# The head's row scaling shared between VectorE and GpSimd

## The reference

```
h = rmsnorm(x, g_mix);  z = h @ w_in                 # w_in: 2048 x 5632
rmsnorm(x, g) = x * rsqrt(mean(x*x) + 1e-6) * g
mixer A: 16 heads x 64, three dilated windows, mixed by their softmax denominators
mixer B: 16 query heads / 4 kv heads x 64, window 128, with a sink logit per head
x1 = x + concat(A * silu(gate_a), B * silu(gate_b)) @ w_out
x2 = x1 + (p @ w_ple) * sigmoid(rmsnorm(x1, g_ple) @ w_pg)
y  = rmsnorm(x2, g_final)                            # and the keys and values of both mixers
```

## Time and profile before

| what | value |
|---|---|
| median of 3 runs | 2525.15 us (2521.14 to 2525.96) |
| the profiled execution's own time | 2522.66 us |
| its span in the trace | 2520.9 us |
| mean granted clock of PE | 0.989 of full speed |
| PE busy | 2427.4 us (96%) |
| DVE busy | 861.3 us (34%) |
| ACT busy | 634.7 us (25%) |
| POOL busy | 812.4 us (32%) |

### The profile page before, as it was taken

How to read it: one execution, slowest core, us unless ns; L and a number is a source line. 1 busy time by engine, 2 the same in 40 slices (tenths; PEclk the granted TensorE clock), 3 DMA queues, 4 the chain that set the end, 5 groups by cost and what they waited for, 6 DMA issues and landing times.

```text
span 2520.9 us, 41153 instructions
## 1 busy us (share of the span) xinstructions
PE 2427.4 (96%) x16473; PEld 2260.6 (90%) x16473; DVE 861.3 (34%) x2199; ACT 634.7 (25%) x1748; POOL 812.4 (32%) x858
## 2 busy tenths in 40 slices
PE   5999999999999999999999999999999999999986
PEld 4998888888888999888888899999999998999986
DVE  7022333333333322445545535251221253222242
ACT  6022222222222222333555510130000032112211
POOL 1322222222222222222212223333333233454896
PEclk9999999999999999999999999999999999999998
DMA  5232222223222214444434445352332343333675
GB/s 182 72 115 94 88 90 96 82 84 109 86 89 91 89 58 126 124 128 138 146 114 142 124 148 161 112 179 86 99 97 79 117 157 106 111 105 109 181 227 175
DMA packets 349110, 297.26 MB, mean 118 GB/s; under 512 B 22191, under 2 KB 314263, under 8 KB 347631
## 3 DMA queue, kind: packets, MB, share of 16 engines
q1 hardware_dynamic: 312197, 253.37, 33.1%
q10 hardware_dynamic: 36723, 41.26, 4.8%
HBM read 228.43 MB, written 66.12 MB: 117 GB/s over the span
## 4 chain that ended last, share of the span: by engine, by line
PE 82%; DVE 5%; POOL 5%; DMA 4%; ACT 1%; issue 1%; SPq 1%; DVEq 0%; POOLq 0%; ACTq 0%
PE psum L935 22%; PE psum L937 22%; PE psum L936 22%; PE psum L739 3%; PE psum L755 3%; PE psum L767 3%; POOL w_lo L708 3%; POOL w_hi L706 2%; DMA s_ring<-in_cache_a_k 2%; PE psum L795 1%; PE psum L823 1%; PE psum L810 1%; DVE x_n L1381 1%; DMA w_raw<-in_w_ple 1%; DVE s_prod L1474 1%
## 5 line engine op out<-in xcount | busy, mean ns | idle before, releaser
L935 PE MATMUL psum<-act_hi,w_hi 128*128 128x344 f32 x4032 | 1323.5, 328 | 21.0 <-POOL w_lo L708 11.3
L937 PE MATMUL psum<-act_hi,w_lo 128*128 128x344 f32 x4032 | 1290.7, 320 | 0.0
L936 PE MATMUL psum<-act_lo,w_hi 128*128 128x344 f32 x4032 | 1290.0, 320 | 0.0
L935 PEld LDWEIGHTS psum<-act_hi,w_hi 128*128 128x128 f32 x4032 | 762.0, 189 | 35.6 <-POOL w_lo L708 14.6
L706 POOL CAST w_hi<-w_raw 128x512 fp32r<-128x512 f32 (+1 forms) x390 | 246.9, 633 | 1652.7 <-PE psum L937 1505.1
L936 PEld LDWEIGHTS psum<-act_lo,w_hi 128*128 128x128 f32 x4032 | 761.6, 189 | 0.2
L937 PEld LDWEIGHTS psum<-act_hi,w_lo 128*128 128x128 f32 x4032 | 760.8, 189 | 0.0
L708 POOL TENSOR_TENSOR w_lo<-w_raw,w_hi 128x512 fp32r<-128x512 f32 (+1 forms) x390 | 503.8, 1292 | 31.2
L1404 DVE COPY prob_t<-psum 128x512 f32<-128x512 f32 (+2 forms) x96 | 53.5, 558 | 468.9 <-PE psum L767 468.9
L1155 ACT ACTIVATE prob_t<-psum 128x512 f32<-128x512 f32 (+2 forms) x96 | 47.1, 491 | 352.5 <-PE psum L767 352.5
L1161 ACT ACTIVATE prob<-prob,mx 128x256 f32<-128x256 f32 (+7 forms) x128 | 98.4, 770 | 147.0 <-DVE mx L1432 147.0
(11 more groups left out here) (192 smaller groups left out, 1900.0 us busy)
## 6 DMA issues: line engine op xcount, KB each, us to landing
w_raw<-in_w_in SPq DMA_DIRECT2D x208, 256.0 KB, 3.1
w_raw<-in_w_pg SPq DMA_DIRECT2D x94, 256.0 KB, 2.9
w_raw<-in_w_out SPq DMA_DIRECT2D x64, 256.0 KB, 2.7
z_scratch<-stage ACTq DMA_DIRECT2D x72, 172.0 KB, 1.8
h_scratch<-h_row ACTq DMA_DIRECT2D x16, 516.0 KB, 2.7
x_in<-in_x_prompt SPq DMA_DIRECT2D x8, 1024.0 KB, 4.9
zq<-z_scratch SPq DMA_DIRECT2D x32, 256.0 KB, 4.0
bias<-in_c_biasa SPq DMA_DIRECT2D x16, 512.0 KB, 4.2
```

Source lines behind the costliest of these rows:

```text
L935: pe.matmul(psum[:, bank, 0:T3], hi_w, hi_a[:, k, rows], start=(k == 0), stop=False, skip_group_check=True)
L936: pe.matmul(psum[:, bank, 0:T3], hi_w, lo_a[:, k, rows], start=False, stop=False, skip_group_check=True)
L937: return pe.matmul(psum[:, bank, 0:T3], lo_w, hi_a[:, k, rows], start=False, stop=stop, skip_group_check=True)
```

## The change

POOL takes columns 1408 to 2047 of each row tile's scaling and does it in two instructions. The first multiplies `x_in` by `g_row` into `x_n`; it waits for `x_squared`, since ACT writes its junk there. The second multiplies that by the inverse root, and waits for the DVE's `dve_chain` count of that tile's fourth small step. Both count `x_shared`. DVE's scaling keeps columns 0 to 1407. SP's load of tile i and PE's turning of a tile now wait for both counts. In POOL's program tiles 0, 1 and 2 stand ahead of weight group 0; tile 3 stands ahead of group 2, tile 4 ahead of group 3, and tiles 5 to 8 ahead of group 4.

```diff
+X_SHARE = 11 * P
@@ SP: loads of the row tiles
                 if i >= 2:
                     sp.wait_ge(sem("x_normed"), i - 1)
+                    sp.wait_ge(sem("x_shared"), 2 * (i - 1))
                 sp.dma_start(x_in[0:n, i % 2, :], x_p[r0:r0 + n, :] if i < 8 else x_s).then_inc(sem(f"x_loaded{i % 2}"), 16)
@@ POOL
+            def x_share(i):
+
+                r0, n = ROW_TILES[i]
+                pool.wait_ge(sem("x_squared"), i + 1)
+                pool.tensor_tensor(x_n[0:n, i % 2, X_SHARE:D], x_in[0:n, i % 2, X_SHARE:D], g_row[0:n, X_SHARE:D], ALU.mult).then_inc(sem("x_shared"), 1)
+                pool.wait_ge(sem("x_shared"), 2 * i + 1)
+                pool.wait_ge(sem("dve_chain"), 4 * i + 4)
+                pool.tensor_scalar(x_n[0:n, i % 2, X_SHARE:D], x_n[0:n, i % 2, X_SHARE:D], small[0:n, 18 + i:19 + i], None, ALU.mult).then_inc(sem("x_shared"), 1)
+
+            pool.wait_ge(sem("consts"), 64)
+            for i in range(3):
+                x_share(i)
             for g, (what, i, k, n) in enumerate(GROUPS):
+                for x in {2: (3,), 3: (4,), 4: (5, 6, 7, 8)}.get(g, ()):
+                    x_share(x)
@@ PE, x_turn
                 pe.wait_ge(sem("x_normed"), i + 1)
+                pe.wait_ge(sem("x_shared"), 2 * i + 2)
@@ DVE
-                dve.scalar_tensor_tensor(x_n[0:n, i % 2, :], x_in[0:n, i % 2, :], small[0:n, 18 + i:19 + i], g_row[0:n, :],
+                dve.scalar_tensor_tensor(x_n[0:n, i % 2, 0:X_SHARE], x_in[0:n, i % 2, 0:X_SHARE], small[0:n, 18 + i:19 + i], g_row[0:n, 0:X_SHARE],
                                          ALU.mult, ALU.mult).then_inc(sem("x_normed"), 1)
```

## The result

Over 11 runs of each kernel the median went from 2523.43 to 2535.11 us, 11.7 us more; the ratio of the times is 1.0048 with a 95% interval of 1.0038 to 1.0059. The forecast was 2534.2 us, slower, which is 9 us above the median of the three runs of before (2525.15 us). The profiled execution of the changed kernel took 2536.74 us, with a span of 2534.9 us, a granted clock of 0.986, PE busy 2427.6 us and POOL 854.5 us (42 more than before).

What follows compares the result with a forecast made beforehand. DVE bounds the head and PE the rest; the late x 3 costs tile 3 8.5 us, later tiles win nothing back, and PE passes tile 8 +9.4 late, taken as +9: 2525.15 + 9 = 2534.2 us, range 2526 to 2539.

Steps and rivals of the forecast that it cites:

- the held load: SP's queue: x 3 stands behind g 2, which waits for group 0's split behind tile 2; issued 8.9 us later.
- The main case: Head ends later through the late x 3 and mutual waits: +9 us, own range +6 to +11, chance 0.62.
- POOL is dearer: Rival: POOL's one-input product costs 1.54 us, or POOL gets ahead of DVE's scaling; +13 or about +12 us, chance 0.18.
- signs of being wrong: x 3 before 28 us, tiles at 5.2 us, POOL's scaling above 1 us, PE's clock lower behind the longer pause.
- The queue step: SP's order x 2, g 2, x 3: x 3 issued at 31.85 instead of 22.96 us, tile 3 scaled 8.5 late.
- The mutual wait: DVE instructions with two SBUF operands and POOL instructions exclude each other to the end; five tiles take 30.0 us against 29.5.
- the guess who goes first: Both scalings are released by the same count; DVE taken to go first, POOL following 1.65 us later.
- The mis-sized term: POOL's per-row scaling of 640 columns, taken near the cast as 0.75 us, bounded by 0.67 and 1.54.
- The rounding: Scaling starts in the tile-by-tile sum were said to be rounded up by some hundredths each, so +9.4 became +9 us.
- nothing comes back behind the head: PE behind tile 8's turning has almost no idle time, so a head d us later makes the kernel d us longer.
- The faster rival: DVE stays the only bound and x 3 is issued by 27.7 us; at best 6.3 us less, 2519 us, chance 0.05.
- The rival without mutual waits: DVE's parts run beside POOL's, x 3 issued at 28.4 us, five tiles win back 3.5; +1, 2526 us, chance 0.14.

Runs made afterwards that it cites:

- waits_only: Kernel before with POOL's program in the new order, POOL only waiting where its nine shares would stand; 2529.54 against 2521.37 us, ratio 1.0028, head +5.9 us.
- sp_order: Changed kernel with SP loading x 3 ahead of g 2, and g 2 and g 3 behind x 4; ratio to the kernel before 1.0034, head +6.0 us.
- sp_two: Changed kernel with x 3 loaded ahead of g 2 and POOL's second instruction a broadcast two-tensor product; ratio to the kernel before 1.0018, head +3.4 us.
- share256: Changed kernel with 256 instead of 640 columns on POOL; 2529.12 us against 2521.37 of the kernel before, ratio 1.0038, head +7.6 us.
- one_product: Changed kernel with x 3 loaded ahead of g 2 and POOL's first product (by g_row) left out; ratio to the kernel before 1.0009, head +1.3 us.
- two_tensor: Changed kernel with POOL's per-row scaling written as a two-tensor product, inverse root broadcast; ratio to the kernel before 1.0046, head +9.7 us.

## Why the prediction was right, step by step

The direction and the first mechanism, the held load, were right. The main case was right only in part: the head's +12.4 lies above that case's own +6 to +11 and beside the rival "POOL is dearer" (+13), and one of its signs of being wrong, POOL's scaling above 1 us, came true. That the forecast of 2534.2 us stands within 1 us of the measured 2535.11 is luck: the change is 11.7 us and not 9, and the median of before fell from 2525.15 to 2523.43 with more runs.

| step | forecast | measured |
|---|---|---|
| DVE's scaling, 1408 columns | 1.65 | 1.68 |
| POOL's first product, 640 columns | 1.54 | 1.53 |
| POOL's scaling, 640 columns | 0.75 (0.67 to 1.54) | 1.89 |
| x 3 issued | 31.85 | 32.82 |
| tile 3 scaled | 41.0 | 42.27 |
| tiles 4 to 8, start to start | 6.6, 6.6, 5.2, 6.4, 5.2: 30.0 | 5.8, 6.7, 7.4, 5.9, 5.4: 31.1 |
| PE past tile 8 | 75.4 | 78.36 |
| the head | +9.4, taken as +9 | +12.4 |

- The queue step was right in place and nearly in size, and waits_only and sp_order show it as a cause of its own.
- The mutual wait came as forecast where it mattered for the sum: L1383 held in six tiles by 0.5 to 0.8 us, POOL's scaling held by DVE's in all but tile 1. As a rule it was too wide: POOL's per-row scaling holds no DVE instruction (0.22 and 1.69 us in the rows of 16.84 and 17.48). Two readings behind the rule were off as well. The 0.71 us by which DVE's scaling of 15.27 is stretched is not the overlap, which is 0.90 (15.27 to 16.17). And "whichever came first" is not what 18.86 and 18.88 say, where DVE's instruction is recorded 0.02 us ahead and is the one that waits. Right was the guess who goes first: where both are released by the same count, DVE is 0.13 to 0.15 us ahead (26.98 and 27.11).
- The mis-sized term is POOL's scaling, 1.89 us where the sum had 0.75, above even the upper bound that I drew. I took the nearest row to be the cast, since both read one tensor; the multiplication by a per-row scalar costs more than the product of two tensors. Behind DVE's scaling 1.75 us of it are left (28.66 to 30.41) and not 0.75, on tiles 2, 3, 4, 5 and 7: 5 us more in the sum. With the broadcast form at 1.25 us the head is past tile 8 at 75.67.
- The rounding hid part of this. From L1364's end to the scaling the sum goes by 0.6 us where the earlier trace rows give 0.42, on the same five tiles: 0.9 us in all, and not some hundredths. With both put right the forecast's own sum would be about +13.5, an estimate; measured are +12.4, or +13.0 from tile 0's scaling.
- One detail was wrong without changing the sum: in tiles 4 and 5 I had L1364 held until the product's end. In fact it slips in between the split and the product, takes 0.77 us, and the scaling is held instead (2.55).
- Tile 6 took 7.4 us instead of 5.2. Its load was issued at 52.44, when POOL's scaling of tile 4 had ended, and not at 50.05, and it took 5.6 us instead of 4.9. Here the mis-sized term went through the loads.
- That nothing comes back behind the head was right. The pause did lower the clock, which the forecast named as a sign of being wrong: PE had been idle for 11.65 us, the granted clock of 30 to 40 us was 0.50 (1.2 of 2.4 GHz) and that of 40 to 50 us 0.54, where before had 0.73 and 1.00. Tile 3 took 3.63 us to turn (before 3.31) and tile 5 3.32 (before 1.97), where tile 4 took 1.94. It cost nothing all the same: PE still stood idle before it turned tiles 6 and 7 (0.59 us, and 1.10 in the row of 71.55), so POOL's end set these and not PE. (The 7.3 of 10 us that the forecast gives for the end of the present pause is the stretch of 50 to 60 us in the earlier trace rows; that of 40 to 50 us has 7.53.)
- The faster rival: x 3 would have had to be issued before 27.7 us. sp_order issues it at about 22.8 and is still 6.0 us late in the head, so the held x 3 was not all that kept it from coming. The rival without mutual waits (2526 us) falls with the held rows and with the time.

## What to carry to other kernels

When work is put into another engine's program, look at what stands behind it there: here a weight split, a buffer's release, and then a load in a queue that had nothing to do with the moved work. That cost as much as the work itself, and one line in SP's order gave it back. And a share moved to POOL saves DVE's time only where POOL's products and casts find a place beside DVE instructions with at most one operand in SBUF, and where POOL ends its share in time for the next load; 5.5 us of possible gain with 640 columns became 2 at best in the head, with fewer columns, the shorter form and a third buffer.

## What the runs showed of the hardware

- POOL's multiplication by a per-row scalar took 1.89 us for 640 columns and the same product written with a broadcast tensor 1.25; the product of two full tensors took 1.53 (640), 1.26 (512), 0.99 (384) and 0.72 us (256), 2.1 ns a column. The Trainium skill (GPSIMD Engine Reference, Elementwise — side-by-side cycle accounting) has one-input bodies at 1.03 cycles an element, well below two-input ones; 1.89 against 1.53 us says the opposite for this instruction, and the measurement decides.
- Who holds whom depends on POOL's instruction. Its products and casts held DVE's instructions with two SBUF operands: 0.22 us became 0.97 (25.58, changed kernel), 1.68 became 2.55 (48.06), and 0.22 became 0.39 beside a cast (38.32, sp_two). Its multiplication by a per-row scalar held none: in the changed kernel, sp_order (two places), share256 and one_product nine such DVE instructions began 0.5 us or more after it was free to run and before its end, and all took their usual time. The same product in broadcast form did hold them (0.60, two_tensor).
- An instruction of 8 partitions took as long as one of 128: POOL's product 1.55 and 1.54 us, DVE's scaling 1.67 and 1.69.
- A held POOL instruction has a little less left than its full time when the other ends: two_tensor's ends 1.11 us behind DVE's scaling (15.01 + 2.69 against 14.90 + 1.69) where it takes 1.25 alone. The rest must have been done during the wait; what it is, no run here shows.
- Not tried: DVE's scaling with its second operand outside SBUF, which would have taken the mutual wait away and left both engines' work in place.
